# Differential attention: three slots of score banks, maps turned in two passes of one bank, latent and context tiles of a pair in one group

## The reference

```python
def block(j, qb):
    logits = jnp.einsum("bqhmd,bkhmd->bhmqk", qb, k).astype(jnp.float32) * scale
    p = jax.nn.softmax(logits, axis=-1)
    a = (p[:, :, 0] - lam * p[:, :, 1]).astype(v.dtype)
    return jnp.einsum("bhqk,bkhd->bqhd", a, v)

def finish(o, n):
    return (rms_norm_2(o, subln_g) * (1.0 - lambda_init)).reshape(b, n, MIX_WIDTH_2)
```

## Time and profile before

| | us |
|---|---|
| median of the timed runs | 3364.74 |
| the profiled execution | 3358.62 |
| its span in the trace | 3356.8 |
| PE busy in it | 3171.4 |
| VectorE busy | 1507.1 |
| ScalarE busy | 1340.1 |
| GpSimd busy | 1163.9 |

### The profile page before, as it was taken

The page is one execution under the profiler, slowest core; times in us unless marked ns, Lnnn a source line. Parts: engine busy times, 40 slices in busy tenths (PEclk is TensorE's granted clock), DMA queues, the critical chain, the costliest instruction groups (busy, mean ns, idle before and its releaser), DMA issues. The chain is left out here.

```text
span 3356.8 us, 51850 instructions
## 1 busy us (share of the span) xinstructions
PE 3171.4 (94%) x20662; PEld 2610.3 (78%) x20662; DVE 1507.1 (45%) x2679; ACT 1340.1 (40%) x2452; POOL 1163.9 (35%) x649
## 2 busy tenths in 40 slices
PE   7989999999989999989999999999999988799998
PEld 6857788877667888878887888877888877588787
DVE  4963443117844443131377310268323348832473
ACT  4353333223433333243366322267232237723463
POOL 4531444445414444434201322243234422225302
PEclk9998999999999999989999999999999999899999
DMA  4345232323452333232100111110112200013102
GB/s 149 115 159 188 82 99 97 98 83 118 157 196 80 97 98 98 94 99 84 32 2 14 57 63 61 54 48 14 53 61 85 85 20 1 8 51 109 43 2 76
DMA packets 81957, 262.42 MB, mean 78 GB/s; under 512 B 11952, under 2 KB 13360, under 8 KB 81712
## 3 DMA queue, kind: packets, MB, share of 16 engines
q1 hardware_dynamic: 81712, 259.05, 23.8%
HBM read 239.60 MB, written 2.10 MB: 72 GB/s over the span
## 5 line engine op out<-in xcount | busy, mean ns | idle before, releaser
L175 PE MATMUL ps<-hs,head 128*128 128x512 f32 x4176 | 870.0, 366 | 16.0 <-PEq L95 4.4
L175 PE MATMUL ps<-hs,WS 128*128 128x512 f32 x4176 | 862.8, 364 | 5.8 <-POOL WS L156 5.7
L175 PEld LDWEIGHTS ps<-hs,head 128*128 128x128 f32 x4176 | 715.1, 190 | 160.4 <-issue 14.7
L175 PEld LDWEIGHTS ps<-hs,WS 128*128 128x128 f32 x4176 | 714.1, 189 | 139.4 <-POOL WS L156 7.9
L156 POOL TENSOR_TENSOR WS<-W,WS 128x1024 fp32r<-128x1024 f32 x168 | 408.5, 2432 | 614.5 <-ACT WS L148 614.5
L156 POOL TENSOR_TENSOR head<-W,head 128x1024 fp32r<-128x1024 f32 x165 | 398.0, 2412 | 594.4 <-ACT head L148 594.2
L148 ACT CAST WS<-W 128x1024 fp32r<-128x1024 f32 x168 | 176.1, 1048 | 351.0 <-PE ps L175 324.1
L1635 ACT ACTIVATE prob<-ps,low 128x768 f32<-128x768 f32 (+4 forms) x320 | 223.4, 700 | 179.4 <-DVE low L1707 177.1
L1707 DVE TENSOR_REDUCE low<-ps 128x1 f32<-128x768 f32 (+4 forms) x320 | 216.6, 702 | 94.9 <-PE ps L1150 90.5
L148 ACT CAST head<-W 128x1024 fp32r<-128x1024 f32 x165 | 172.7, 1047 | 198.2 <-PE ps L175 198.1
L1150 PE MATMUL ps<-kk,qq 64*128 64x256 f32 (+3 forms) x2064 | 213.7, 333 | 39.2 <-ACT prob L1367 23.1
(11 more groups left out here) (295 smaller groups left out, 3931.8 us busy)
## 6 DMA issues: line engine op xcount, KB each, us to landing
W<-in_stream_dram SPq DMA_DIRECT2D x432, 512.0 KB, 3.5
swap<-prj SPq DMA_DIRECT2D x168, 64.0 KB, 2.1
band<-in_bias_band_dram SPq DMA_DIRECT2D x8, 512.0 KB, 3.6
prj<-prj SPq DMA_DIRECT2D x64, 64.0 KB, 2.8
xT<-in_x_dram SPq DMA_DIRECT2D x4, 512.0 KB, 8.3
W<-in_stream_dram SPq DMA_DIRECT2D x1, 2048.0 KB, 13.3
xT<-turned SPq DMA_DIRECT2D x8, 256.0 KB, 7.0
out_dram<-xT SPq DMA_DIRECT2D x8, 256.0 KB, 2.7
```

The lines of the kernel that those rows point to most:

```text
L175: last = pe.matmul(out, a(i), b(j), start=start and n == 0, stop=stop and n == 2)
```

## The change

- **Scores.** Unit u = 2x + hd (a map of tile x) takes two banks of the six 0 to 5, in turn by u mod 3, context tiles too. The scores of tile x wait for the exponentials of units up to 2x - 2: the first map of the tile before.
- **Transposes.** All go to bank 6, in two passes: the first four blocks (front), then, of a latent tile and after the value product of the tile before it, the last two (back). Each pass waits until the pass before is copied out.
- **ACT's order** in a step: front copy of tile x - 2, the two exponentials of x, the scaled copy of x - 3 (before: of x - 4, first in the step), then loads and squares.
- **DVE's order** in a step: first maximum, reciprocals and weight of the tile before, second maximum, combination, back copy (before: reciprocals and weight, both maxima, copy, combination).
- **Groups.** In the differential layer a group holds the four latent and the two context tiles of a pair, with 768 queries. Clamps, squares and sums are 768 wide, one tile earlier. POOL's low halves wait for `combined` of the tile before in place of `weight_known`.

```diff
+        backs = lambda n: sum(not W.small(x) for x in range(n))
+        turns = lambda n: n + backs(n)
+        parts = lambda x: [W.columns(x)[i:i + 4] for i in range(0, W.size(x) // P, 4)]
+        turned_parts = lambda x, i: M.ps[:, 6, 0:len(parts(x)[i]) * P].rearrange("p (x n) -> p x n", n=P)
+        def banks(x, hd):
+            b = 2 * ((2 * x + hd) % 3)
+            return M.ps[:, b:b + 2, :].rearrange("p b n -> p (b n)")
...
             @block.gpsimd
-                            if n == min(1, last - 1):
+                            if n == 1:
                                 pool.wait_ge(queries_high, g)
-                                if y:
-                                    pool.wait_ge(weight_known, y)
+                                pool.wait_ge(combined, y)
                                 operands.q_low_plain(g % 2, p, q_cols).then_inc(queries_low, 1)
...
             @block.tensor
+                def turn(y, i):
+                    if y + i:
+                        pe.wait_ge(front_copied, y + i)
+                    if backs(y) and not i:
+                        pe.wait_ge(back_copied, backs(y))
+                    for j, sc in enumerate(parts(y)[i]):
+                        last = pe.transpose(M.ps[:, 6, j * P:j * P + P], prob[:, (2 * y + 1) % (2 * ring), sc:sc + P],
+                                            M.const[:, C_ID:C_ID + P])
+                    last.then_inc(turned, 1)
...
                         if x:
-                            pe.wait_ge(exped, max(1, W.exps_ahead(x)))
+                            pe.wait_ge(exped, 2 * x - 1)
...
                     if 2 <= x < X + 2:
+                        pe.wait_ge(combined, x - 1)
+                        turn(x - 2, 0)
                     if x >= 3:
                         y = x - 3
                         p, nb = works[y][1], len(W.blocks(y))
-                        pe.wait_ge(turn_copied, y + 1)
+                        pe.wait_ge(front_copied, y + 1)
+                        pe.wait_ge(back_copied, backs(y + 1))
...
+                    if 2 <= x < X + 2 and not W.small(x - 2):
+                        turn(x - 2, 1)
...
             @block.scalar
+                    if 2 <= x < X + 2:
+                        y = x - 2
+                        act.wait_ge(turned, turns(y) + 1)
+                        if y >= 2:
+                            act.wait_ge(weighted, y - 1)
+                        nc.scalar.copy(probT[:, y % 2, 0:len(parts(y)[0]), :], turned_parts(y, 0)
+                                       ).then_inc(front_copied, 1)
...
             @block.vector
+                    if 2 <= x < X + 2 and not W.small(x - 2):
+                        y = x - 2
+                        dve.wait_ge(turned, turns(y + 1))
+                        nc.vector.tensor_copy(probT[:, y % 2, 4:, :], turned_parts(y, 1)).then_inc(back_copied, 1)
...
+                if kind == 2:
+                    tiles += [context(m) for m in range(QT, NT)]
+                    groups = [(p, (0, N), (0, N), tiles) for p in range(PAIRS2)]
+                elif go_on:
...
-                    first_rows(nc, M, FirstRows(operands, (0, S), (0, N)))
+                    first_rows(nc, M, FirstRows(operands, groups[0][1], (0, N)))
```

More of the change, by code:

```diff
@@ L1266, in difference_attention @@
     X, works, groups = W.X, W.works, W.groups
-    tails = lambda n: sum(W.tail(x) > 0 for x in range(n))
     ends = W.start[1:]
@@ L1273, in difference_attention @@
         prob, probT = sbuf(nc, mem, "prob", [P, 2 * ring, n_keys]), sbuf(nc, mem, "probT", [P, 2, n_keys // P, P])
[L1274 removed]
+        clamped, scaled = sbuf(nc, mem, "clamped", [P, 2, N]), sbuf(nc, mem, "scaled", [P, N])
         low, total, inv = (sbuf(nc, mem, name, [P, 2 * X]) for name in ("low", "total", "inv"))
@@ L1322, in _ @@
                         if x:
-                            pe.wait_ge(exped, max(1, W.exps_ahead(x)))
-                        operands.scores(pe, lambda hd: W.scores(M, x, hd), g % 2, g % 2, m * P // 2, keys
-                                        ).then_inc(scored, 1)
+                            pe.wait_ge(exped, 2 * x - 1)
+                        operands.scores(pe, lambda hd: banks(x, hd), g % 2, g % 2, m * P // 2,
+                                        [(keys[0][0], 0, CTX)] if W.small(x) else keys).then_inc(scored, 1)
                         if x < 3:
@@ L1397, in _, with largest @@
             def _(dve):
+                def largest(x, hd):
+                    u = 2 * x + hd
+                    nc.vector.tensor_reduce(low[:, u:u + 1], scores(x, hd), AX_X, ALU.max, negate=True
+                                            ).then_inc(maxed, 1)
                 for x in range(X + 8):
+                    if x < X:
+                        dve.wait_ge(scored, x + 1)
+                        largest(x, 0)
                     if 1 <= x <= X:
@@ L1406, in _ @@
                                                        ).then_inc(weight_known, 1)
[L1407 to L1420, removed]
+                    if x < X:
+                        largest(x, 1)
                     if 1 <= x <= X:
@@ L1429, in _ @@
                             dve.wait_ge(squared, 2 * g + 2)
-                            src = clamped[:, g % 2] if lag == 6 else scaled
+                            src = clamped[:, g % 2] if lag == 5 else scaled
                             nc.vector.tensor_reduce(dst[:, W.start[g]:ends[g]],
```

74 lines of the change are left out of this document (24 added, 50 removed).

## The result

| | before | after |
|---|---|---|
| median of eight timed runs each, us | 3362.82 (3360.26 to 3365.22) | 3378.53 (3372.09 to 3385.75) |
| ratio, 95% interval | | 1.0041 (1.0030 to 1.0052) |
| the profiled execution, us | 3358.62 | 3383.49 |
| its span | 3356.8 | 3381.7 |
| first to last S of the stage | 173.2 | 184.5 |

The change makes the kernel slower. The medians are 15.7 us apart (0.47%), the ratio of the runs gives 0.41%, about 13.8 us; +6.0 was forecast. 3378.53 lies 0.5 above the upper end of the range.

A forecast was written before the change was run, and what follows sets the result against it. A chain of waits, 4.29 us a latent tile, was taken to bound the stage, no engine being full. Stage +4.6, start +0.2 and tail +1.2 gave +6.0: 3364.6 profiled, 3370.7 timed, range 3352 to 3378.

The forecast's parts named there:

- by hand: Worked timetable of one middle pair's six tile steps in the differential stage, POOL's blocks included: 22.73 us.
- by hand without blocks: The same pair's timetable with POOL holding nothing up on VectorE: 20.05 us.
- Loops (a) to (c): Latent-step wait loops: scores behind the first exponential 3.40, front copy ahead of it 3.41, single transpose bank 3.5 us a tile.
- The first pair: First of the stage's eight pairs, with four filler products as before, first step 4.85: 24.2 us in all.
- The block: POOL's 1.81 us low halves hold the weight W of n2 and n3 on VectorE, each about 1.6 us; chance 0.43.
- margins: How far behind POOL's start the weight W starts: 0.20 us in n2, 0.13 in n3.
- The rivals by which W gets ahead: The weight starts before POOL once (3364.5 us, chance 0.22) or both times (3358.3 us, chance 0.20).
- the nearly free port: Rival: POOL and VectorE meeting at SBUF costs next to nothing, -12.8 us, 3352; chance 0.08.
- The clock: Rival: PE idle behind blocked VectorE falls to 1.2 GHz, 1.9 us over a latent step, six give 3382; chance 0.05.
- The tail: Stage's end: a single chain of clamp, two squares and a reduction, each 768 wide: +1.2 us.
- The grouping: Context tiles grouped with their pair's latent tiles carry the preceding latent tile's PE work; sixteen loads become eight wider ones.
- The 0.2 at the start: At the stage's start the high queries are 768 wide: 0.2 us more.

The follow-up runs named there:

- e5: The changed kernel with POOL's low halves cut into 384-column pieces and moved, high halves a tile earlier, clamp behind the weight; ratio 0.9978.
- e4: The kernel before with only its groups changed to four latent and two context tiles of a pair; ratio 1.0034.
- e2: The changed kernel with POOL filling zeros in place of computing the low halves from the second pair on; ratio 0.9975.
- e3: The changed kernel's slots, transpose passes and orders with the groups of before; ratio 0.9979.
- e7: The changed stage with the groups of before, plus POOL's low halves and clamp cut or placed to fit; ratio 0.9960.
- e9: The changed kernel run once more, unchanged, with a second trace; ratio 1.0036.
- e1: The changed kernel with POOL's low halves waiting for the combination one tile later; ratio 0.9997.
- e6: The changed kernel with reciprocals and weight moved behind the second maximum on VectorE; ratio 0.9985.
- e8: e7 with the two squares on ACT one step apart; ratio 0.9958.

## Why the prediction fell short, step by step

| step of a pair, us | n0 | n1 | n2 | n3 | n4 | n5 | sum |
|---|---|---|---|---|---|---|---|
| by hand | 3.40 | 3.40 | 3.55 | 4.87 | 4.69 | 2.82 | 22.73 |
| after, pairs 2 and 5 | 3.39 | 3.39 | 3.55 | 4.95 | 4.69 | 2.86 | 22.83 |
| after, pairs 3, 4, 6, 7 | 3.39 | 3.39 | 3.55 | 4.95 | 6.27 | 2.81 | 24.36 |
| by hand without blocks | 3.40 | 3.40 | 3.55 | 3.45 | 3.42 | 2.83 | 20.05 |
| e5 | 3.40 | 3.39 | 3.55 | 3.56 | 3.53 | 2.86 | 20.29 |

- **Loops (a) to (c): right,** within 0.02 us in the first three steps of pairs 2 to 7.
- **The first pair: right in its sum by luck.** It took 4.74 3.40 5.24 3.47 4.37 2.79, 24.0 us, where 4.85 3.40 3.55 4.87 4.69 2.82, 24.2, was worked out. The step from n2 is 1.7 longer, a term the sum had at nothing: in the new order TF stands behind the filler products of the third tile, so that S to TF is 3.07 instead of 1.25. It is 5.24 or 5.25 in every kernel with the new order, and 4.29 or 4.30 in before and e4. The two steps behind it are 1.7 shorter than by hand: the first of this pair's two blocks costs nothing (e2, without blocks, has 5.24 3.48 there too), the second 0.8 (4.37 against 3.56), with W at 1.34 and 1.03. And the 4.85 of the first step is not the fillers' own price: they took 3.68 there at the lower clock, 1.99 at the full clock in e5, where the step is 3.39.

```profile
2754.75 1.31 PE L1150 MATMUL ps<-kk,qq 64*128 64x512 f32 x12 [0.15 <-ACT prob L1375]
...
2755.99 1.99 PE L184 MATMUL ps<-const 128*128 128x256 f32 x8
...
2757.82 0.60 PE L1326 MATMUL ps<-const,prob 128*128 128x128 f32 x4
```

- **The block: right,** in place, number and length: 14 times, 1.61 and 1.68 in pairs 2 to 7, margins 0.21 and 0.16 for the 0.20 and 0.13 by hand, and the M0 of n4 and the transposes wait for VectorE. The rivals by which W gets ahead (0.22, 0.20) did not occur, nor the nearly free port. e2 and e5 are the proof by removal: 22.8 becomes 20.3 when POOL's instructions no longer read SBUF, and again when they are cut and moved.
- **The clock: right as a mechanism, wrong as an alternative.** It stood as a rival at 0.05, in place of the forecast. It came on top of it, in four pairs of six: 1.5 us each, 6.1 in all (the rival had 1.9 a tile). With 0.7 of hand-offs over six pairs, and 0.1 less at the two ends, that is the 6.7 by which 184.5 exceeds 177.8. This is the step of the prediction that failed: the sum had nothing for the clock, and it costs 6.1 us. I had written that PE would wait less than the 18% of before; in the pair of after it idles more (28.60 of 40 us busy, for 32.94), and in longer pieces.
- **The tail: +2.8 for +1.2.** From the last S to the last R it is 7.77 us (2931.09 to 2938.86) for 7.00 before: the last context tiles still carry a latent tile's value product of 1.50. From there to the end of the last sum it is 4.73 for 2.99, the chain of 768-wide instructions in a row, each waiting for the one ahead (another 0.3 lies in what follows it):

```profile
2938.86 0.37 ACT L1382 ACTIVATE prj<-ps,inv 128x128 f32<-128x128 f32 x1 [0.87 <-PE ps L1353]
2939.31 0.83 POOL L1315 TENSOR_SCALAR clamped<-prj 128x768 f32<-128x768 f32 x1 [13.01 <-ACT prj L1382]
2940.17 0.84 ACT L1395 ACTIVATE clamped<-clamped 128x768 f32<-128x768 f32 x1 [0.94 <-POOL clamped L1315]
2940.92 0.83 ACT L1398 ACTIVATE scaled<-prj 128x768 f32<-128x768 f32 x1
2941.78 0.95 DVE L1435 TENSOR_REDUCE near<-clamped 128x6 f32<-128x768 f32 x1 [4.79 <-ACT scaled L1398]
2942.65 0.94 DVE L1435 TENSOR_REDUCE far<-scaled 128x6 f32<-128x768 f32 x1
```

- **The grouping** I had taken as a means of carrying transposes under the context tiles. e3 and e4 show it as the part that costs: with the old groups the same stage is 0.21% faster than before, with its own POOL work fitted 0.40%. With POOL fitted in both, e5 against e7, the grouping costs 6.1 us. The two halves of the change don't add: -9.3 and +12.0 by the timed runs, but +15.7 together, because only together do the 768-wide low halves meet an order in which they don't fit.
- **In all,** stage and tail are 14.1 where the forecast had 4.6 + 1.2: 6.7 more in the stage, 1.6 more in the tail. The 0.2 at the start lies ahead of first S and can't be read.

**What stays open** is why the clock falls where it does. In after, PE's wait of 1.96 or 1.97 comes with a low stretch in pairs 3, 4, 6 and 7; in pairs 2 and 5 the same wait does not, and in e9 it is again four of six. Here pair 5:

```profile
2860.09 0.63 PE L1326 MATMUL ps<-const,prob 128*128 128x128 f32 x4 [1.97 <-DVE probT L1429]
2860.56 1.50 PE L1353 MATMUL ps<-vtok,probT 128*128 128x128 f32 x12
```

Between 2766 and 2885 us PE never waits above 1.31 us at a time in e1, e2, e5 and e6, and these show no low stretch; after and e4, with waits of 1.96 and 2.15, show four and six. But e3, e7 and e8 have one each near the first context tiles, where PE had waited 1.70, 0.98 and 1.17 at most in the 8 us ahead of it, and before has one at 2904.1, with waits of up to 0.83 ahead. That longer idle pieces are the cause is argued, not shown: no run changed PE's idle pieces and nothing else.

## What to carry to other kernels

Before a GpSimd instruction that reads SBUF is made wider or moved, look for the longest stretch of VectorE's queue that holds no instruction with two SBUF inputs: the piece must fit into it, whatever GpSimd's share of busy time, and cutting it in two may be worth more than the instruction saved. Try each half of a combined change alone; here one half gained and the other lost more. And where a block leaves the tensor engine idle for longer pieces than before, give the fall of its clock a price on top of the block, not only in its place.

## What the runs showed of the hardware

- A VectorE instruction of one column (W, 0.22 us alone) took up to 1.68 us, for it waited for all of a 1.81 us POOL instruction that had begun 0.16 before it. The end is exact: 0.01 to 0.03 behind POOL's end, in after, e1 and e6. The block goes the other way too: in before a clamp of 512 columns that started 0.08 behind a C of 256 (2879.99) took 0.87 instead of 0.61.
- C of 768 columns (1.01 alone) ended 0.80 or 0.81 behind POOL's end wherever it was held: the earlier trace rows, e1, e5 and e6. An excess of 0.1 in such a row doesn't mean a shared port, but that all of C except its first 0.2 waited for POOL's end.
- The stages ahead, the same code in all kernels, hold 102.4 to 136.5 us of lower clock from one profile to the next. A span is no measure of a change of 0.3%; the stage's own rows are.
